# Two-block decoder kernel: the feed-forward activation turned by one VectorE transposition and an exchange through HBM

## The reference, cut to what matters

```python
D_FF = -(-8 * D_MODEL // (3 * 256)) * 256      # 5632
h = rms_norm(x, norm_ffn[l])
x = x + (jax.nn.silu(h @ w_ffn_gate[l]) * (h @ w_ffn_up[l])) @ w_ffn_down[l]
```

## Time and profile before

| | |
|---|---|
| median of 3 runs | 1954.85 us (1953.87 to 1955.96) |
| the profiled execution, its own time | 1954.96 us |
| its span in the profile | 1953.5 us |
| TensorE busy | 1947.0 us, 100% |
| VectorE busy | 1369.8 us, 70% |
| ScalarE busy | 1021.1 us, 52% |
| GpSimd busy | 0.2 us |
| HBM traffic | 349.47 MB read, 2.11 MB written |
| weight loads | 326 of 1 MB, 4.8 us from issue to landing |

### The profile page before, as it was taken

One profiled execution on the slowest core, in us unless ns is written; L12 is line 12 of the kernel. 1 busy time (PEld: TensorE's weight loads), 2 busy tenths in 40 slices (PEclk: granted clock), 3 DMA queues, 4 the chain that ended last, 5 costly groups with the idle time before them and its releaser, 6 DMA issues.

```text
span 1953.5 us, 26280 instructions
## 1 busy us (share of the span) xinstructions
PE 1947.0 (100%) x10316; PEld 1668.4 (85%) x10316; DVE 1369.8 (70%) x2046; ACT 1021.1 (52%) x1497; POOL 0.2 (0%) x4
## 2 busy tenths in 40 slices
PE   9999999999999999999999999999999999999999
PEld 7889988988888888898888888888888888888887
DVE  6756777987557677898687877588666444666654
ACT  5645555675456754575565755444444334444442
POOL 0000000000000000000000000000000000000000
PEclk9999999999999999999999999999999999999999
DMA  8554325555543555546543345555555555555563
GB/s 326 178 189 173 130 100 184 181 203 179 194 151 130 183 185 191 182 168 217 194 149 146 110 171 179 198 186 192 193 187 186 210 195 194 193 194 187 185 232 108
DMA packets 51711, 353.28 MB, mean 181 GB/s; under 512 B 5652, under 2 KB 7196, under 8 KB 9860
## 3 DMA queue, kind: packets, MB, share of 16 engines
q1 hardware_dynamic: 50016, 348.84, 49.0%
q10 hardware_dynamic: 1572, 2.75, 0.4%
HBM read 349.47 MB, written 2.11 MB: 180 GB/s over the span
## 4 chain that ended last, share of the span: by engine, by line
PE 92%; DVE 5%; ACT 1%; issue 1%; DMA 0%; SPq 0%; ACTq 0%; DVEq 0%
PE bank L1167 92%; DVE WL L2106 2%; ACT WH L1599 0%; DVE AR L2283 0%; DVE ft L2881 0%; DMA mu_acc<-in_sgu 0%; DVE AR L2396 0%; DVE XP L2279 0%; DVE AR L2393 0%; DVE XP L2381 0%; PE bank L1312 0%; DVE AR L2272 0%; DVE AR L2307 0%; DVE AR L2306 0%; ACT XP L1730 0%
## 5 line engine op out<-in xcount | busy, mean ns | idle before, releaser
L2106 DVE TENSOR_TENSOR WL<-raw,WH 128x1024 fp32r<-128x1024 f32 x649 | 784.9, 1221 | 339.6 <-ACT WH L1599 336.4
L1599 ACT ACTIVATE WH<-raw 128x1024 fp32r<-128x1024 f32 x649 | 682.9, 1057 | 609.8 <-PE bank L1167 603.5
L1167 PE MATMUL bank<-XP,WH 128*128 128x512 f32 (+2 forms) x2096 | 668.2, 393 | 0.4 <-DVE XP L2381 0.2
L1167 PEld LDWEIGHTS bank<-XP,WL 128*128 128x128 f32 x2016 | 378.5, 188 | 80.6 <-issue 0.7
L1167 PE MATMUL bank<-WH,FP 128*128 128x512 f32 x1408 | 435.0, 390 | 0.1
L1167 PE MATMUL bank<-XP,WL 128*128 128x256 f32 (+1 forms) x2016 | 409.6, 279 | 0.1
L1167 PEld LDWEIGHTS bank<-XP,WH 128*128 128x128 f32 (+1 forms) x2096 | 328.9, 188 | 7.6 <-issue 1.4
L1167 PEld LDWEIGHTS bank<-WH,FP 128*128 128x128 f32 x1408 | 264.4, 188 | 55.7 <-DVE WL L2106 1.0
L1167 PE MATMUL bank<-WL,FP 128*128 128x512 f32 x704 | 274.1, 389 | 0.0
L1167 PE MATMUL bank<-WH,AP 128*128 128x512 f32 x704 | 217.0, 389 | 0.0
L1167 PEld LDWEIGHTS bank<-WL,FP 128*128 128x128 f32 x704 | 132.2, 188 | 27.3
(11 more groups left out here) (330 smaller groups left out, 1722.1 us busy)
## 6 DMA issues: line engine op xcount, KB each, us to landing
raw<-in_W SPq DMA_DIRECT2D x326, 1024.0 KB, 4.8
out<-XT ACTq DMA_DIRECT2D x8, 256.0 KB, 2.1
raw<-in_W SPq DMA_DIRECT2D x3, 512.0 KB, 6.8
X<-in_x SPq DMA_DIRECT2D x3, 512.0 KB, 12.8
AR<-rv SPq DMA_DIRECT2D x1, 1024.0 KB, 5.9
cst<-in_cst SPq DMA_DIRECT2D x1, 899.5 KB, 11.8
raw<-in_W SPq DMA_DIRECT2D x2, 256.0 KB, 4.2
AR<-in_sgu SPq DMA_DIRECT2D x1, 512.0 KB, 6.4
```

What stands on the lines that cost most here:

```text
L1167: return pe.matmul(o, lhsT, rhs, start=start, stop=stop)
L1599: ac.activation(w_slot(WH, s), raw_half(hf), ACT.Copy).then_inc(s_hi, 1)
L2106: tt(w_slot(WL, s), raw_half(pl.half_of[s]), w_slot(WH, s).bitcast(F32), ALU.subtract).then_inc(s_lo, 1)
```

## The change

- "act turned" is one step a group, at position 1, and one instruction: a transposition of 128x1024 from `fu` into a new buffer `fq`. Each 32x32 block stays in its own 32 partitions (a quarter). The columns of `fq` are ordered by the quarter they have to go to.
- GpSimd has a program for the first time: for each group it stores `fq` to a scratch tensor `turn` in HBM (512 KB, two buffers), waits until it has landed, and issues four loads of 128 KB, one for each quarter of `ft`'s partitions. Each takes, for 32 partitions, a piece of 256 floats from each of the four quarters stored.
- "act halves" waits for the four loads (`s_back`) instead of VectorE, reads `ft` in runs of 32 columns, and writes `AP` in the same order as before.
- "x turned" may also stand at positions 3 and 4.

```diff
-        elif at < 5:
-            say("act turned", 4 * (g + FFN_GROUPS[0] * half) + at - 1)
+        elif at == 1:
+            say("act turned", g + FFN_GROUPS[0] * half)
...
-            if half == 0 and g and at in (6, 7, 9, 10, 11, 12, 13, 14) and turned < 16:
+            if half == 0 and g and at in (3, 4, 6, 7, 9, 10, 11, 12, 13, 14) and turned < 16:
...
-        sg, fu, ft = (sb(n, 1024, at=xp0 + 4 * (4096 + 1024 * i)) for i, n in enumerate(("sg", "fu", "ft")))
+        sg, fu, fq, ft = (sb(n, 1024, at=xp0 + 4 * (4096 + 1024 * i)) for i, n in enumerate(("sg", "fu", "fq", "ft")))
+        ft_blocks = ft[:, :].rearrange("p (q f i) -> p f q i", q=4, f=8)
...
                     elif what == "act halves":
-                        ac.wait_ge(s_ftr, 4 * n + 4)
-                        ac.activation(AP_[:, 2048 * (n - g0):2048 * (n - g0) + 1024], ft[:, :], ACT.Copy).then_inc(s_ahi, 1)
+                        ac.wait_ge(s_back, 64 * (n + 1))
+                        o = 2048 * (n - g0)
+                        ac.activation(by_quarter(AP_[:, o:o + 1024]), ft_blocks, ACT.Copy).then_inc(s_ahi, 1)
...
                     elif what == "act turned":
-                        g, a = divmod(n, 4)
-                        if a == 0:
-                            dv.wait_ge(*outed(*up_block(g), 1))
-                            if g:
-                                dv.wait_ge(s_ahi, g)
-                        src, dst = (t[:, :].rearrange("p (f t) -> p f t", f=8) for t in (fu, ft))
-                        for b in range(4):
-                            ins = dv.transpose(dst[32 * b:32 * b + 32, :, 32 * a:32 * a + 32],
-                                               src[32 * a:32 * a + 32, :, 32 * b:32 * b + 32])
-                        ins.then_inc(s_ftr, 1)
+                        dv.wait_ge(*outed(*up_block(n), 1))
+                        if n:
+                            dv.wait_ge(s_away, 16 * n)
+                        dv.transpose(fq[:, :].rearrange("p (q f i) -> p f q i", q=4, f=8),
+                                     fu[:, :].rearrange("p (f q i) -> p f q i", f=8, q=4)).then_inc(s_ftr, 1)
                     elif what == "act halves":
                         dv.wait_ge(s_ahi, n + 1)
                         o = 2048 * (n - g0)
-                        tt(AP_[:, o + 1024:o + 2048], ft[:, :], AP_[:, o:o + 1024].bitcast(F32),
-                           ALU.subtract).then_inc(s_alo, 1)
+                        tt(by_quarter(AP_[:, o + 1024:o + 2048]), ft_blocks,
+                           by_quarter(AP_[:, o:o + 1024]).bitcast(F32), ALU.subtract).then_inc(s_alo, 1)
...
+        def pool_program():
+
+            for g in range(sum(FFN_GROUPS)):
+                to = dr["turn"][g % 2]
+                po.wait_ge(s_ftr, g + 1)
+                if g >= 2:
+                    po.wait_ge(s_back, 64 * (g - 1))
+                po.dma_start(to, fq[:, :]).then_inc(s_away, 16)
+                po.wait_ge(s_away, 16 * (g + 1))
+                if g:
+                    po.wait_ge(s_alo, g)
+                for r in range(4):
+                    src = to[:, 256 * r:256 * (r + 1)].rearrange("(q j) c -> j q c", q=4)
+                    po.dma_start(ft[32 * r:32 * r + 32, :].rearrange("j (q c) -> j q c", q=4), src).then_inc(s_back, 16)
...
+    dr["turn"] = nc.dram_tensor("turn", (2, 128, 1024), F32, kind="Internal").ap()
```

More of the change, by code:

```diff
@@ L822, in sem @@
             return ctx.enter_context(nc.semaphore(name))
-        pe, dv, ac, sp = nc.tensor, nc.vector, nc.scalar, nc.sync
+        pe, dv, ac, sp, po = nc.tensor, nc.vector, nc.scalar, nc.sync, nc.gpsimd
         pl = plan()
@@ L1017, in build, with by_quarter @@
         XT = sb("XT", 4096, at=xp0)
-        sg, fu, ft = (sb(n, 1024, at=xp0 + 4 * (4096 + 1024 * i)) for i, n in enumerate(("sg", "fu", "ft")))
+        sg, fu, fq, ft = (sb(n, 1024, at=xp0 + 4 * (4096 + 1024 * i)) for i, n in enumerate(("sg", "fu", "fq", "ft")))
+        ft_blocks = ft[:, :].rearrange("p (q f i) -> p f q i", q=4, f=8)
+        def by_quarter(t):
+            return t.rearrange("p (f q i) -> p f q i", f=8, q=4)
         def act_part(k, half, low):
@@ L1094, in build @@
         s_ftr, s_ahi, s_alo = (sem("s_" + n) for n in ("ftr", "ahi", "alo"))
+        s_away, s_back = sem("s_away"), sem("s_back")
         s_dnf = sem("s_dnf")
@@ L2948, in sync_program @@
             sp.wait_ge(s_fin, 16 * 8)
+        def pool_program():
[11 more added lines that the diff above has]
+                    po.dma_start(ft[32 * r:32 * r + 32, :].rearrange("j (q c) -> j q c", q=4), src).then_inc(s_back, 16)
         sync_program()
+        pool_program()
         act_program()
```

## The result

The changed kernel takes 1979.12 us (median of 4 runs, 1974.81 to 1982.74) against 1954.97 us before (median of 4, 1953.87 to 1955.96): a ratio of 1.0122, 95% interval 1.0110 to 1.0134. It is slower by 24 us. The forecast was "no change"; what came is the first rival, "the round trip misses the date", which stood at 1972 us and a third of the chances.

What follows compares the result with a forecast made beforehand. The prediction took TensorE to bound the kernel (92% of the chain) and summed 1954.96 - 0.4 + 0.4 + 11 x 0 = 1955.0 us, "no change", with a range of 1953.3 to 1985 us.

Steps and rivals of the forecast that it cites:

- the first rival: Feed-forward exchange: slow issues (1 us each) make the trip 13.1 us, 1.5 us late per group; 1972 us, chance 33%.
- TensorE bounds, and VectorE's relief is worth nothing: Whole kernel: TensorE is 92% of the chain; VectorE's 63 us saved lie beside matmuls, 0 us of the end.
- The date: Last feed-forward group: ScalarE must start AP's high half by 1857.17, 0.74 us after its 1856.43 start; delay x costs 11x.
- The single transposition: VectorE, each group: sixteen transpositions of 6.98 us together become one of 1.17 us, at most 1.22.
- The store: GpSimd's 512 KB store of fq to HBM: 4.4 us to land, bounds 2.7 and 6.9.
- GpSimd's issuing: Exchange loads: three issues of 0.43 us each counted before the last load's landing.
- The second rival: GpSimd's five DMA issues each wait for a VectorE operation of 1.22 us: 53 us, 2008 us, chance 8%.
- Item 4: The four loads back into ft: 3 x 0.43 + 4.4 = 5.7 us, bounds 3.3 and 10.7.
- the trip: Store, four loads and hand-overs through HBM: 10.3 us (6.2 to 17.8) against 11.6 allowed, back 1.3 us early.
- The upper end, 10.7: Upper bound for the four loads: each issue 2.1 us, as long as a small landing, last landing 4.4 us.
- Each us of delay costs one us: Past the high half's latest start, each microsecond of delay is one of TensorE, in each of 11 groups.

Runs made afterwards that it cites:

- the first experiment: Changed kernel without the exchange through HBM: GpSimd issues nothing and the halves of AP are made from fq itself; 1954.65 us, ratio 0.9997 to the kernel before.
- the delays made by copies: Kernel before, with one or three ScalarE copies of ft to a spare buffer ahead of each high half; 1960.86 us (ratio 1.0031) and 2000.56 us (1.0232).
- the thinnest weights: Changed kernel with feed-forward weight loads cut to 64 of 2048 columns (32 KB each); 1953.74 us, one run, no ratio.
- the three-copies kernel: Kernel before, with three ScalarE copies of ft to a spare buffer ahead of the high half in each group; 2000.56 us, ratio 1.0232.
- the one with the wide load: Changed kernel with the exchange's shapes turned round: four stores of 128 KB, then one load of 128 rows of 4 KB; 1979.30 us, ratio 1.0122.

## Why the prediction was right in the dates and wrong in the sum

- **TensorE bounds, and VectorE's relief is worth nothing**: right. VectorE is busy 65.2 us less; the first experiment has all of this relief and a ratio of 0.9997.
- **The date**: right, and the most useful number of the prediction. 1857.17 came from three timelines; in the changed kernel the loss of the last group follows it (1.67 us of delay, 1.79 us lost), the pauses of nine others do, and the delays made by copies follow it at 0.4 and 2.7 us (0.5 and 2.68 lost).
- **The single transposition**: 1.235 us, where 1.17 and at most 1.22 were predicted. Right but for 0.015 us.
- **The store**: 3.2 us landed against 4.4 taken. Over-estimated by 1.2.
- **GpSimd's issuing**: 0.55 us each, the same within 5 ns for all 44 loads, where 0.43 was taken. The second rival (issuing held up by VectorE) did not occur. The Trainium skill's "SBUF — State Buffer", in its list of who interferes with whom, names copy and tensor_scalar, not tensor_tensor, as what starves descriptor writing, and the trace agrees: 552 to 557 ns beside tensor_tensor and transpositions. The landings, which would show late descriptors, were 3.0 and 3.2 us with the thinnest weights, with VectorE as busy as ever.
- **The four loads: this step failed.** Item 4 took 3 x 0.43 + 4.4 = 5.7 us; it was 1.64 + 7.86 = 9.5 us in the last group, with a median landing of 6.9 over all. With it the trip went from 1.3 us ahead of the date to 1.7 us behind it, and "no change" to 24 us. The trip grew by less than these 3.8 us, as the store was over-estimated. The range, which reached to x = 2.7 us a group, holds the time, but more by the width given to the first rival than by the sum. The row taken for it was that of 128 KB landing behind a few other loads at the start of the kernel. The upper end, 10.7, held. The wrong argument behind the choice was the one against the first rival, that the DMA engines are busy by half only the earlier trace rows: that is the mean of 110 us. In the 10 us of the exchange they are busy for 97%, since the store and the loads fill the gaps that the strip of the earlier trace rows shows between two weight loads.
- **The first rival** had the right mechanism and almost the right trip (13.1 us against 13.25), but by another term: slow issuing in place of a slow landing. That its trip came so close is luck. Its 17 us lacked the lower clock behind long pauses (4.9 us) and a slower start behind each pause: one of 2.39 us in the three-copies kernel costs 2.68, of which 0.16 is the modelled end of a matmul and 0.13 the slower start, 1.4 us over 11 groups.
- **"Each us of delay costs one us"** held for the pauses themselves, up to 2.7 us of delay. Behind some of those from 1.84 us on the lower clock cost 1.63 us more, which the prediction had not counted.

## What to carry to other kernels

When work goes off a full engine's path, the question is not how much busy time it frees but at which date the result must be back; take that date from the timelines of the waiting queues, and compare it with the whole trip. Price a small DMA by the traffic in its own few microseconds, and not by the mean: beside 1 MB loads a 128 KB load took twice the time that it took with 32 KB loads beside it (6.9 us and 3.2). Here issuing the waiting step one position later was worth as much as taking away three quarters of the traffic beside the exchange.

## What the runs showed of the hardware

TensorE's clock fell behind pauses. In the changed kernel, around its first one (start, us, one or two matmuls; the distance of two starts counts):

```profile
1296.94 0.62 PE L1173 MATMUL bank<-WH,FP 128*128 128x512 f32 x1 [3.03 <-DVE WL L2113]
1297.36 0.63 PE L1173 MATMUL bank<-WL,FP 128*128 128x512 f32 x1
...
1300.35 0.74 PE L1173 MATMUL bank<-WH,FP 128*128 128x512 f32 x2
1300.93 0.40 PE L1173 MATMUL bank<-WL,FP 128*128 128x512 f32 x1
1301.16 0.62 PE L1173 MATMUL bank<-WH,FP 128*128 128x512 f32 x2
```

From 1296.94 to some 1300.4 us two matmuls start 0.43 us apart, the 1.2 GHz level; from 1300.93 on 0.23, the 2.4 GHz level. Over the feed-forward parts of the changed kernel, the one with the wide load and the two with copies there are 44 such pauses: behind the 26 of up to 1.79 us the clock stayed up, behind 14 of the 18 from 1.84 to 3.03 us it fell for about 3.4 us. Why it stayed up behind the other four, of 1.93, 2.16, 2.49 and 2.39 us, is open. Since the same pause is followed sometimes by the one and sometimes by the other, this fits the wider spread of the changed kernel's runs (8 us from lowest to highest, 2 us before); that it is the cause was not tried.
